# When the routing steps of a streaming-encoder kernel are dealt between its expert gathers, and in what order the first group routes

## The reference, cut to what matters

```python
def peer_tokens(x, wq, keys, u, v):
    n = x.shape[0]
    q = jnp.einsum('nd,dc->nc', x, wq).reshape(n, PEER_HEADS, 2, PEER_HALF)
    s1 = jnp.einsum('nhd,hkd->nhk', q[:, :, 0], keys[0]).astype(F32)
    s2 = jnp.einsum('nhd,hkd->nhk', q[:, :, 1], keys[1]).astype(F32)
    v1, i1 = lax.top_k(s1, PEER_TOPK)
    v2, i2 = lax.top_k(s2, PEER_TOPK)
    cand = (v1[..., :, None] + v2[..., None, :]).reshape(n, PEER_HEADS, PEER_TOPK * PEER_TOPK)
    cv, ci = lax.top_k(cand, PEER_TOPK)
    e = (jnp.take_along_axis(i1, ci // PEER_TOPK, axis=-1) * N_KEYS
         + jnp.take_along_axis(i2, ci % PEER_TOPK, axis=-1))
    g = jax.nn.softmax(cv, axis=-1)
    ...
    act = jax.nn.gelu(jnp.einsum('nd,nhkd->nhk', x, ue).astype(F32))
    w = (g * act).astype(x.dtype)
    return jnp.einsum('nhk,nhkd->nd', w, ve)
```

## Time and profile before

| what | value |
|---|---|
| median of 3 runs | 4367.41 us |
| the profiled execution, its span | 4370.94 us, 4369.0 us |
| TensorE busy | 2459.9 us (56%) |
| VectorE busy | 2473.4 us (57%) |
| GpSimd busy | 1359.4 us (31%) |
| ScalarE busy | 475.6 us (11%) |
| gathers (queue q0) | 1208.03 MB, 67.2% of the 16 DMA engines' span |
| chain that ended last | DMA 33%, TensorE 22%, VectorE 15% |

### The profile page before, as it was taken

One profiled execution on the slowest core, in us unless ns is written; L12 is line 12 of the kernel. 1 busy time (PEld: TensorE's weight loads), 2 busy tenths in 40 slices (PEclk: granted clock), 3 DMA queues, 4 the chain that ended last, 5 costly groups with the idle time before them and its releaser, 6 DMA issues.

```text
span 4369.0 us, 34811 instructions
## 1 busy us (share of the span) xinstructions
PE 2459.9 (56%) x11906; PEld 1023.5 (23%) x11906; DVE 2473.4 (57%) x6235; ACT 475.6 (11%) x1311; POOL 1359.4 (31%) x1257
## 2 busy tenths in 40 slices
PE   7998997780675656433347476566134334334333
PEld 4465443340231222110013142222001001001000
DVE  3212611159565557887656545577986555555555
ACT  1000112111220100010012010001101000000000
POOL 0000210000344334334334334343144444444443
PEclk9966996895787777756578677788556656656655
DMA  3001033202899999779999999999299999999999
GB/s 103 20 10 50 20 118 136 87 10 87 354 415 390 401 395 417 315 299 417 417 417 416 368 387 395 418 413 397 110 421 419 415 418 417 419 419 419 417 420 374
DMA packets 241776, 1347.65 MB, mean 308 GB/s; under 512 B 33456, under 2 KB 47096, under 8 KB 94144
## 3 DMA queue, kind: packets, MB, share of 16 engines
q0 software_dynamic: 165888, 1208.03, 67.2%
q1 hardware_dynamic: 73408, 135.08, 8.4%
q10 hardware_dynamic: 2304, 2.32, 0.2%
HBM read 1318.14 MB, written 27.21 MB: 308 GB/s over the span
## 4 chain that ended last, share of the span: by engine, by line
DMA 33%; PE 22%; DVE 15%; POOL 7%; issue 5%; ACT 2%; SPq 0%; DVEq 0%; POOLq 0%; ACTq 0%
DMA M<-in_peer_uv,M 31%; PE yp L1436 12%; POOL M L1048 7%; DVE M L1679 5%; PE ab L1390 3%; DVE strips L1701 1%; PE ab L1254 1%; PE c L1369 1%; DMA M<-in_w_out 1%; PE d L1277 1%; ACT gel L1213 1%; DVE M L1550 1%; DVE M L1554 1%; DVE M L1557 1%; PE ef L1424 1%
## 5 line engine op out<-in xcount | busy, mean ns | idle before, releaser
L1048 POOL DMA_INDIRECT M<-in_peer_uv,M x1152 | 1279.8, 1111 | 2210.8 <-PE yp L1436 1749.0
L1679 DVE SCALAR_TENSOR_TENSOR M<-M 128x1024 f32<-128x1024 f32 x1152 | 1406.5, 1225 | 844.4 <-DMA M<-in_peer_uv,M 820.5
L1436 PE MATMUL yp<-M,strips 128*32 128x512 f32 x4608 | 933.3, 952 | 1484.2 <-DVE strips L1701 1482.6
L1436 PEld LDWEIGHTS yp<-M,strips 128*32 128x32 f32 x4608 | 161.6, 147 | 2122.4 <-DVE strips L1701 1726.4
L332 PE MATMUL z<-M 128*128 128x512 f32 x1008 | 442.3, 596 | 1.4 <-PEq L104 1.0
L1213 ACT ACTIVATE gel<-gel 128x4 f32<-128x4 f32 x288 | 59.2, 206 | 1941.1 <-DVE gel L1690 1941.1
L1390 PE MATMUL ab<-M 128*128 128x512 f32 x576 | 266.4, 613 | 1.3 <-ACT M L1169 1.3
L332 PEld LDWEIGHTS z<-M 128*128 128x128 f32 x1008 | 189.6, 191 | 226.9 <-issue 226.9
L1424 PE MATMUL ef<-ident,M 128*32 128x128 f32 x2304 | 79.8, 303 | 182.8 <-ACT M L1209 182.8
L414 POOL TENSOR_SCALAR small<-small 128x8 f32<-128x8 f32 x27 | 6.1, 227 | 520.5 <-DVE small L483 520.5
L1390 PEld LDWEIGHTS ab<-M 128*128 128x128 f32 x576 | 109.4, 197 | 150.6 <-issue 149.0
(11 more groups left out here) (201 smaller groups left out, 2343.6 us busy)
## 6 DMA issues: line engine op xcount, KB each, us to landing
M<-in_peer_wq SPq DMA_DIRECT2D x12, 2048.0 KB, 28.5
M<-in_peer_uv,M POOLq DMA_INDIRECT x1152, 10.7
M<-in_w_in SPq DMA_DIRECT2D x7, 2048.0 KB, 9.1
M<-in_w_out SPq DMA_DIRECT2D x24, 512.0 KB, 22.6
M<-in_x_prompt SPq DMA_DIRECT2D x16, 512.0 KB, 7.2
x_scratch<-M SPq DMA_DIRECT2D x9, 512.0 KB, 7.8
xts_scratch<-M SPq DMA_DIRECT2D x9, 512.0 KB, 15.4
M<-xts_scratch SPq DMA_DIRECT2D x9, 512.0 KB, 11.6
```

The source lines that it names most:

```text
L1048: nc.gpsimd.indirect_dma_start(ring[n % NR], None, a["peer_uv"], bass.IndirectOffsetOnAxis(ap=idxH[:, t % 6, s // 4, s % 4:s % 4 + 1], axis=0)
L1436: last = nc.tensor.matmul(yp[32 * j:32 * j + 32, 512 * c:512 * c + 512], strips[:, n % 2, j, :], ring[(4 * n + j) % NR][:, D + 512 * c:D + ...
L1679: nc.vector.scalar_tensor_tensor(out=row, in0=row, scalar=1.0, in1=xrep[:, s % 4, :], op0=ALU.mult, op1=ALU.mult, accum_out=dots[:, t % 2, ...
```

## The change

1. `due_steps()` keeps a separate time for each of the two engines. A step that uses TensorE is placed at the time TensorE is free and advances only that time (its cost over 6.2); likewise VectorE (over 3.4); no step is placed ahead of the one before it. `hsq` and `hsum` now stand in pairs.
2. Group 0 takes its passes tile by tile (`block_of`: pass `i` is key set `i % 4` of tile `i // 4`), and the choice for its tile 0 stands right behind pass 4. All four `peer_wq` blocks and key sets of group 0 have places of their own and are loaded early.
3. The choices for tiles 1 and 2 of group 0 are taken out of the part before the first dot and put at the head of the list that is dealt to batches 0 to 88.
4. The ring starts at another slot, so that the first four gathers wait only for the choice of tile 0, and the other five also for the last scores.
5. In `weigh`, the product of the 32-column pattern and half the gate is now made ahead of the wait for the tanh, and one operation behind it makes the strips (before: a 128x4 and a 128x128 operation behind the wait).
6. At the start SyncE issues two loads before it waits for its own store, and waits for it later.

```diff
-            for i in range(GT + 1):
-                if i < GT:
-                    out.append((0, 0, "hsq", g, i))
-                if i >= 1:
-                    out.append((0, 0.6, "hsum", g, i - 1))
+            for i in range(GT):
+                out += [(0, 0, "hsq", g, i), (0, 0.6, "hsum", g, i)]
...
+            choice = [[(0, 1.15, "rcand", g, i, p) for p in range(CAND)] +
+                      [(0, 0, "rexp", g, i), (0, 0.6, "rgate", g, i), (0, 0, "rmove", g, i)] for i in range(GT)]
...
-            for i in range(GT):
-                out += [(0, 1.15, "rcand", g, i, p) for p in range(CAND)]
-                out += [(0, 0, "rexp", g, i), (0, 0.6, "rgate", g, i), (0, 0, "rmove", g, i)]
-            return out
+                if g == 0 and i == 4:
+                    out += choice[0]
+            return out, choice[1:] if g == 0 else choice
+
+        def block_of(g, i):
+
+            return (i % 4, i // 4) if g == 0 else (i // GT, i % GT)
...
-                pe_us, dve_us, at = 0.0, 0.0, []
-                for s in front_steps(g):
-                    at.append(max(pe_us / 6.0, dve_us / 3.2))
-                    pe_us, dve_us = pe_us + s[0], dve_us + s[1]
+                steps, choice = front_steps(g)
+                steps = steps + [s for c in choice for s in c]
+                if g == 1:
+                    late = [s for c in front_steps(0)[1] for s in c]
+                    steps = late + steps
+                pe, dve, at = 0.0, 0.0, []
+                for s in steps:
+                    now = max([at[-1] if at else 0.0] + ([pe] if s[0] else []) + ([dve] if s[1] else []))
+                    at.append(now)
+                    if s[0]:
+                        pe = now + s[0] / 6.2
+                    if s[1]:
+                        dve = now + s[1] / 3.4
...
-            ring = [M[:, 2 * i * D:2 * (i + 1) * D] for i in range(NR)]
+            ring = [M[:, 2 * i * D:2 * (i + 1) * D] for i in (4, 5, 6, 7, 8, 0, 1, 2, 3)]
...
-                pool.wait_ge(q_mm, 4 * GT)
                 for n in range(NR):
+                    if n == 4:
+                        pool.wait_ge(s_mm, 4 * GT)
                     gather(n)
...
+                    link(nc.vector.tensor_tensor(exg[:, :, :], bc(e32[:, :].unsqueeze(1), [P, 4, 32]),
+                                                 bc(g[:, 3, :].unsqueeze(2), [P, 4, 32]), ALU.mult))
                     dve.wait_ge(gel2, n + 1)
-                    link(nc.vector.scalar_tensor_tensor(out=g[:, 0, :], in0=g[:, 2, :], scalar=1.0, in1=g[:, 3, :],
-                                                        op0=ALU.add, op1=ALU.mult))
                     if n >= 2:
                         dve.wait_ge(uv_free, n - 1)
-                    nc.vector.tensor_tensor(strips[:, n % 2], bc(e32[:, :].unsqueeze(1), [P, 4, 32]),
-                                            bc(g[:, 0, :].unsqueeze(2), [P, 4, 32]), ALU.mult).then_inc(strip_done, 1)
+                    nc.vector.scalar_tensor_tensor(out=strips[:, n % 2], in0=bc(g[:, 2, :].unsqueeze(2), [P, 4, 32]),
+                                                   scalar=1.0, in1=exg[:, :, :], op0=ALU.add, op1=ALU.mult
+                                                   ).then_inc(strip_done, 1)
```

46 lines of the change are left out of this document (27 added, 19 removed).

## The result

Four runs of the changed kernel took 4225.2 to 4245.17 us, median 4231.13; the kernel before, beside them, 4367.51 (four runs, 4367.24 to 4374.39). The ratio is 0.9689, 95% interval 0.9663 to 0.9714: 3.1% faster. The forecast was 4217 us. The profiled execution took 4225.2 us, its span 4223.3.

A forecast was written before the change was run, and what follows sets the result against it. The gather part was taken as DMA bound at 10.06 us a batch. From 4369.0 us, 80 (start) and 139 (heaps) go and 69 are given back: span 4219, median 1.6 less, 4217; range 4140 to 4300.

The forecast's parts named there:

- the 98 dense batches: Batches with fox, heads, routing or sample steps: 1230 us, 93 above the floor of 1137; wrong under 1180 or over 1280.
- Start: Before the first tanh: tile 0's choice behind pass 4 brings it to 1035 us, 80 earlier; bounds 70 and 88.
- Heaps: Batches 63 and 168, 69.9 and 89.0 us with heaped choice work: 139 us of waiting goes.
- Choice batches: VectorE at the DMA's pace: 10.4 us each for batches 1 to 18, 10.35 for 60 to 89, 10.15 in group 2.
- Fox 1: Group 1's fox stage, 13 batches: 157 us at 12.1 each, plus 10 us of idle DMA for its load, 167 us.
- Fox 2: Group 2's fox stage, 17 batches: floor 181 us, five batches with two steps, 193 us.
- Heads and routing: Stages of groups 1 and 2: heads 1 136 us, routing 1 216, heads 2 132, routing 2 240.
- Samples: Group 2's sample stage, 9 batches: floor 119 us, loss 27 as before, 146 us.
- Absorbed: Rival: dense stages lose no more than the earlier 58 us, choice batches run at 10.1 us; 4162 us; chance 0.25.
- Worst-like: Rival: all 98 dense batches take 11.84 us, other bytes (63 MB, 152 us) on top; 4299 us; chance 0.2.
- Slower by the clock: Rival: TensorE falls to the lower clock in the dense stages; with half of them so, 4470 us; chance 0.04.
- the change doesn't do what it says: Rival: tile 1's gathers could come to wait for its choice; given nothing of its own; no change, chance 0.01.

The follow-up runs named there:

- e1: Kernel before with only the new dealing rule (separate engine times); first group, `weigh` and load order as before: 4288.45 us, ratio 0.9810.
- e2: Changed kernel with group 2 alone dealt by the old rule (max of the two sums): 4274.03 us, ratio 0.9769.
- e5: Changed kernel with key, value and decay loads of groups 1 and 2 issued early, in batches 1 and 62: 4196.8 us, ratio 0.9603.
- e11: Changed kernel with `match_replace` left out of the choice, so values are not the reference's: 4222.53 us, ratio 0.9650.
- e3: Changed kernel with the old `weigh`, no product ahead of the tanh: 4240.5 us, ratio 0.9699.
- e6: Changed kernel with a longer pad behind the samples' loads and two pads before the routing of groups 1 and 2: 4210.12 us, ratio 0.9625.
- e7: Changed kernel with early key, value and decay loads, longer pads at samples and before routing, sample steps over more batches: 4182.28 us, ratio 0.9568.
- e8: Changed kernel with half the output and routing projection matmuls of groups 1 and 2 left out (values not the reference's): 4233.22 us, ratio 0.9689.
- e9: e7 with its pads moved: four behind the samples' loads, four between the residual-row and output-weight load and its first use: 4196.8 us, ratio 0.9602.

## Why the prediction was right, point by point

The forecast case held: first tanh, stages and last third add up to 4223.3 against 4219, and the 98 dense batches took 1236.9 us against 1230. The total is nearer than its parts deserve. Of the dense stages, fox 1, the samples and routing 2 came 9, 9 and 13 us over their forecasts, fox 2, routing 1, heads 2 and heads 1 11, 7, 3 and 2 under; that they nearly cancel is luck.

By each stage's own bytes (GB/s x us of its window, over 417) the time above the floor is, with what I had given in brackets: fox 1 20 (23), heads 1 10 (10), routing 1 6 (10), fox 2 0 (12), samples 41 (27), heads 2 9 (4), routing 2 12 (7), 98 us in all (93). Batches 19 to 22 hold 20 of it, 113 and 114 13, 118 and 119 15, 134 and 135 9: over half in four long batches and those right behind them.

- **Start.** 1032.6 against 1035, by two errors that cancel. The choice put pass 5 back by 31.8 us, not 34.2. The lower clock cost 2.4 us, where I took 7, and nothing is seen of the 2 us for the early loads; the last scores came at 1013.75, 34.2 us later than before, not 43.2. Then 18.8 us passed to the first tanh where I had 12.2: the spreading began 3.0 us after the last scores and its second copy waited 3.9 us more.
- **Heaps.** Gone, in e1 and after alike; e2 brings the one of group 2 back.
- **Choice batches.** Batches 1 to 18 took 10.08 us each, not 10.4; 60 to 89 10.36 (10.35 forecast); the last choices 10.24 (10.15). By my own signs batches 1 to 18 went the absorbed way: 10.1 us a batch, and VectorE busy 92% of the time (167.04 of 181.5 us). The DMA share of 1.0 is missed (0.97) for the idle stretch right behind the first tanh, which e5 fills. The second is right for the wrong reason: I put it down to VectorE without slack, and e11's stages show that it had slack. Part of this slack is in the dealing: by `due_steps()` of after a batch carries 3.5 choice pieces, in group 2 3.1, not 3.7 and 3.3, so VectorE needed 9.9 us and not 10.1. Of the 310.8 us, 9 are over 30 x 10.06; 4 us of them are other bytes (1.6 MB on the hardware queue).
- **`weigh`.** I saved 0.14 us a batch; 0.2 are saved, and what arrives is within the noise (e3).
- **Fox 1.** 175.7 against 167. Three terms are off. The load wait: I forecast 25 to 50 us for the batch (37.4 measured) and charged 10 us of idle DMA; but all the idling in the stage came to 19 us (e5). The floor: I counted 5.4 MB beside 13 batches' gathers, and the stage moved 10.5 (65.0 in all), so its floor is 156 us and not 144; the decay rows of the other heads come in it too, and 2.3 MB more of gathers. The two-step batches: I gave them 13 us, and they cost nothing. The batch pair of the earlier trace rows is no limit: the other twelve took 11.1 in e5 at a DMA share of 1.01, less than my 12.1.
- **Fox 2.** 181.9 against 193, on its floor (417 GB/s). I had five batches with two fox steps and 12 us for them; by `due_steps()` there are three, and nothing is lost in them.
- **Heads and routing.** 133.8 (136), 209.0 (216), 128.8 (132), and 252.8 (240). In routing 2 batch 134 stood for the weights and keys of the next passes; e6 took that away and the stage fell to 239.3.
- **Samples.** 154.9 against 146. I had carried over before's loss of 27 us; by the stage's own bytes (47.4 MB, 114 us) it became 41. Two things make it: the wait for a load in batch 113 (30.2 us), and from batch 118 (26.4 us, two score steps, granted clock 0.50) on TensorE's own work; 118 to 121 lose 22 us. That second term I did not have. In e7, with the sample steps dealt more thinly, batches 113 to 125 lose 11.
- **Load rate.** On the earlier trace rows I took a quarter of the bandwidth for the load, 45 us for 4.7 MB. In after the value load, behind that much, landed 36.3 us after its issue. From 1220 to 1240, beside the gathers, the hardware queue (q1) moved 2.32 MB, 116 GB/s or 28% of the whole; only from 1240 to 1246, when the gathers were in, did it get 347. The DMA view of both stretches (packets, MB, share of the engines):

```profile
q0 software_dynamic: 822, 6.00, 72.2%
q1 hardware_dynamic: 826, 2.32, 29.8%
...
q1 hardware_dynamic: 1032, 2.08, 93.7%
```

So the quarter was about right and the time came out shorter because the gathers stopped. The Trainium skill ("DMA: Bandwidth & Descriptors", section "Queues, rings and completion order") has the engines take turns between queues; by equal turns it would be about 23 us (an estimate). This load lies between the two, and I had been right not to count on half.
- **Rate.** I set the rows at 416 to 419 GB/s against 358. That is no conflict: the Trainium skill ("DMA: Bandwidth & Descriptors", section "Bandwidth") gives about 358 GB/s for each core when both cores of a memory domain stream, and this kernel runs on one. No run here has the other core at work.
- **Rivals.** Absorbed (4162; by its own rates the choice batches save 15 us and not 20, so 4167): the 98 dense batches took 100 us over my floor, not 58, though the choices were absorbed. Worst-like (4299) is out, at 1236.9. Slower by the clock is out: it needed 14.1 us a dense batch and they took 12.6 (its `add_v` of 3.6 us is 3.28 in the earlier trace rows; after has 3.64), the fox stages had 0.83 and 0.85, and where e8 lowered the clock to 0.71 the time stayed. But in the samples (0.62) the lower clock is part of the loss, as batch 118 shows. That the change doesn't do what it says is out by e1 and e2.
- **Median.** I took it 1.6 us under the profiled span; it came 7.8 over it (5.9 over the time of that run). The changed kernel spreads over 20 us from run to run, the one before over 7.

What stays open: where the 0.3 us a batch over 10.06 in the choice batches go, beyond the other bytes; whether e11's lower ratio is real; and how much of e7's two remaining stalls could be had, since the one way tried to remove them (e9) brought another elsewhere.
